# The weight remainders under the norms of the output block: made by VectorE before, by GpSimd now

## What is computed

```python
def layer(x, l):
    h = rms_norm(x, g_pre_mix[l]);  proj = h @ w_in[l]          # window attention and HGRN2 branch
    mixed = concatenate([attn, rec]) @ w_o[l]                   # "wo"
    x = x + rms_norm(mixed, g_post_mix[l])
    mk = rms_norm(mem, g_mem[l]) @ w_xk[l]                      # "memk", 256 memory tokens
    mv = rms_norm(mem, g_mem[l]) @ w_xv[l]                      # "memv"
    q = rms_norm(x, g_pre_x[l]) @ w_xq[l]                       # "xq"
    x = x + rms_norm(cross_attention(q, mk, mv) @ w_xo[l], g_post_x[l])
    x = x + rms_norm(conv_ffn(rms_norm(x, g_pre_ffn[l])), g_post_ffn[l])
```

## Time and profile before

| | |
|---|---|
| median of 3 runs | 4506.29 us (4505.77 to 4507.3) |
| the profiled execution | 4508.9 us |
| its span | 4507.1 us |
| TensorE busy | 3715.9 us, 82% of the span |
| VectorE busy | 2318.1 us, 51% |
| ScalarE busy | 1154.8 us, 26% |
| GpSimd busy | 620.7 us, 14% |
| mean granted clock of TensorE | 0.882 of full speed |
| stretch of the output block in question | about 861 to 963 us in layer 0, 3100 to 3201 us in layer 1 |

### The profile page before, as it was taken

How to read it: one execution, slowest core, us unless ns; L and a number is a source line. 1 busy time by engine, 2 the same in 40 slices (tenths; PEclk the granted TensorE clock), 3 DMA queues, 4 the chain that set the end, 5 groups by cost and what they waited for, 6 DMA issues and landing times. The chain is left out here.

```text
span 4507.1 us, 51872 instructions
## 1 busy us (share of the span) xinstructions
PE 3715.9 (82%) x21568; PEld 3497.0 (78%) x21568; DVE 2318.1 (51%) x3358; ACT 1154.8 (26%) x1608; POOL 620.7 (14%) x254
## 2 busy tenths in 40 slices
PE   6777587987897999999667776879868979999995
PEld 5777474876895999999657765658868959999995
DVE  2555555343005777777725554644330066776676
ACT  3222224423013222222132221344230132122211
POOL 1100011111010122122010000111210102112220
PEclk8888688999588999999878887889985889999998
DMA  2000021221310111111010000112214101111110
GB/s 102 34 29 15 29 53 40 87 71 47 131 45 20 43 52 46 45 43 48 15 49 29 29 29 24 44 56 86 65 38 150 33 18 47 47 43 47 47 51 40
DMA packets 57664, 221.74 MB, mean 49 GB/s; under 512 B 7376, under 2 KB 11856, under 8 KB 52048
## 3 DMA queue, kind: packets, MB, share of 16 engines
q1 hardware_dynamic: 56848, 218.13, 15.1%
q10 hardware_dynamic: 576, 0.24, 0.0%
HBM read 198.47 MB, written 14.59 MB: 47 GB/s over the span
## 5 line engine op out<-in xcount | busy, mean ns | idle before, releaser
L215 PE MATMUL ps<-hh,w_hi 128*128 128x344 f32 (+2 forms) x4320 | 1406.6, 326 | 151.2 <-PEq L361 42.0
L216 PE MATMUL ps<-hl,w_hi 128*128 128x344 f32 (+2 forms) x4320 | 1392.8, 322 | 0.0
L217 PE MATMUL ps<-hh,w_lo 128*128 128x344 f32 (+2 forms) x4320 | 1391.7, 322 | 0.0
L200 POOL TENSOR_TENSOR w_lo<-w_raw,w_hi 128x1024 fp32r<-128x1024 f32 x250 | 620.5, 2484 | 3793.1 <-ACT w_hi L192 3793.0
L215 PEld LDWEIGHTS ps<-hh,w_hi 128*128 128x128 f32 x4320 | 823.4, 191 | 169.7 <-issue 96.0
L216 PEld LDWEIGHTS ps<-hl,w_hi 128*128 128x128 f32 x4320 | 823.6, 191 | 1.1
L217 PEld LDWEIGHTS ps<-hh,w_lo 128*128 128x128 f32 x4320 | 822.8, 190 | 0.0
L1857 DVE TENSOR_TENSOR Y<-Y,ps 128x344 f32<-128x344 f32 x1008 | 476.9, 513 | 168.6 <-PE ps L217 168.6
L192 ACT ACTIVATE w_hi<-w_raw 128x1024 fp32r<-128x1024 f32 x276 | 289.6, 1053 | 931.8 <-PE ps L217 803.0
L215 PE MATMUL ps<-f_ghi,w_hi 128*128 128x344 f32 x1056 | 339.7, 322 | 20.0 <-DVE f_glo L1842 20.0
L217 PE MATMUL ps<-f_ghi,w_lo 128*128 128x344 f32 x1056 | 337.5, 320 | 0.0
(11 more groups left out here) (250 smaller groups left out, 4089.7 us busy)
## 6 DMA issues: line engine op xcount, KB each, us to landing
w_raw<-in_w_stream SPq DMA_DIRECT2D x276, 512.0 KB, 3.6
xs_cache<-in_cache_mem_k SPq DMA_DIRECT2D x16, 1024.0 KB, 5.4
xs_cache<-in_cache_mem_v SPq DMA_DIRECT2D x16, 1024.0 KB, 4.9
xT<-in_x_cols SPq DMA_DIRECT2D x1, 4128.0 KB, 16.8
rope_swapped<-Y SPq DMA_DIRECT2D x32, 129.0 KB, 2.3
out_y_cols<-xT SPq DMA_DIRECT2D x1, 4128.0 KB, 11.2
Y<-in_state_hgrn SPq DMA_DIRECT2D x8, 512.0 KB, 3.7
out_hgrn_sample<-Y SPq DMA_DIRECT2D x8, 512.0 KB, 2.6
```

The lines of the kernel that those rows point to most:

```text
L200: nc.gpsimd.tensor_tensor(w_lo[:, SLOT[m], :], w_raw[:, m % RR, :], w_hi[:, SLOT[m], :].bitcast(F32), ALU.subtract).then_inc(lo_done["pool ...
L215: nc.tensor.matmul(out, whi, mhi, start=start, stop=False)
L216: nc.tensor.matmul(out, whi, mlo, start=False, stop=False)
L217: return nc.tensor.matmul(out, wlo, mhi, start=False, stop=stop)
```

## The change

The list of slabs whose remainders VectorE makes becomes empty, and the thirteen places in VectorE's order go. By the condition in `split_lo`, GpSimd now makes every remainder, in the order of the slabs, and `wait_low` asks GpSimd's semaphore everywhere. Loads, high parts, slots and the order of TensorE and ScalarE stay as they are.

```diff
-LOW_ON_DVE = [m for m in range(len(LOADS)) if VISIT["wo", KT - HR, 1] < LOAD_OF.index(m) < VISIT["xq", 0, 0]]
+LOW_ON_DVE = []
...
-                        def low_slab(i):
-
-                            split_lo_dve(dve, LOW_ON_DVE[i] + 1)
-
...
                         root(0)
-                        low_slab(0)
                         normalise(0)
                         add_post(17)
-                        low_slab(1)
                         residual(0, range(0, 4))
                         add_post(18)
-                        low_slab(2)
                         residual(0, range(4, 8))
```

More of the change, by code:

```diff
@@ L1531, in _ @@
                         root(0)
-                        low_slab(0)
                         normalise(0)
                         add_post(17)
-                        low_slab(1)
                         residual(0, range(0, 4))
                         add_post(18)
-                        low_slab(2)
                         residual(0, range(4, 8))
                         add_post(19)
-                        low_slab(3)
                         root(1)
                         add_post(20)
-                        low_slab(4)
                         normalise(1)
                         add_post(21)
-                        low_slab(5)
                         residual(1, range(0, 4))
                         add_post(22)
-                        low_slab(6)
                         residual(1, range(4, 8))
                         add_post(23)
-                        low_slab(7)
                         low(0, range(0, 4))
                         keys(0)
-                        low_slab(8)
                         low(0, range(4, 8))
                         keys(1)
-                        low_slab(9)
                         low(1, range(0, 4))
                         keys(2)
-                        low_slab(10)
                         low(1, range(4, 8))
                         keys(3)
-                        low_slab(11)
                         keys(4)
-                        low_slab(12)
                         keys(5)
```

## The result

| | median | lowest to highest |
|---|---|---|
| before | 4505.45 us | 4504.62 to 4507.3 |
| with the change | 4525.99 us | 4523.14 to 4527.72 |

The ratio is 1.0043 with a 95% interval of 1.0033 to 1.0054, that is 15 to 24 us slower. The medians lie 20.5 us apart, 4525 was predicted.

The account below looks back on a forecast made before the run. VectorE's queue was taken to bound the stretch; eight blocks of 2.1 us, less removed remainders and waits, make the sum 9.3 us late per layer, nothing after: 4506.29 + 18.6 = 4524.9, said as 4525, range 4510 to 4538.

Parts of the forecast that it names:

- What bounds the stretch: Output block, ahead of the third mean: VectorE's queue, without a break from 866.35 to 896.16 but for 0.49 and 0.73 us.
- The price of a block and their count: VectorE loses 2.1 us per GpSimd turn, eight turns ahead of the third mean's sum in each layer.
- That sum: Sum of squares formerly at 882.72: four blocks cost 8.4 us, VectorE waits 1.6 us, the sum is 5.0 us late.
- The next mark: Sum of squares formerly at 895.73, ahead of TensorE's third mean: at 905.0, 9.3 us late.
- What follows the sum: zero: Slabs 46 to 50 and onward: the ring turns in 7.4 to 7.8 us against 7.61, so nothing is added.
- my upper figure: Ring's turn behind a high part: GpSimd's remainder of 2.4 us plus up to 0.4 for a turn of VectorE.
- the median landing of 3.7 us: Ring's turn: from a remainder's end to the next high part 3.9 us, 3.7 of landing and about 0.2 of issue.
- Rival D: TensorE's clock falls to 1.2 GHz more often after more idleness: +6 to +9 us, 4531 to 4542; chance 0.12.
- the sign that the prediction gave for D: In the profile: the chain as forecast, but TensorE's clock under 0.9 in the stretch.
- A (no turn inside a run): VectorE's runs of residuals: GpSimd gets its turn only at a semaphore; 4506.3 + 16 = 4522; chance 0.15.
- B (relief): VectorE's queue gets shorter, GpSimd's remainders fall under reciprocals and waits: mean 4.7 us sooner, twice, 4496.9; chance 0.06.
- C (half of the turns hidden): Half of the eight fall under reciprocals or PSUM reads: 0.9 us for a layer, 4508; chance 0.10.

Follow-up runs that it names:

- e3_tiny: The changed kernel, but GpSimd subtracts only 8 of 1024 elements for slabs 38 to 50; 0.9953 of the kernel before, -21.2 us.
- e2: Against the kernel before, GpSimd makes the remainders of slabs 38 to 44, VectorE keeps those of 45 to 50; 1.0031, +14.0 us.
- e5: The kernel before, but GpSimd also fills its own tile with zeros three times at each of the thirteen moments; 1.0007, +3.2 us.
- e7: The kernel before, but VectorE also makes the remainders of slabs 25 to 32; 0.9971, -13.1 us.
- e8: The kernel before, but VectorE also makes the remainders of slabs 25 to 32, 54 and 59 to 66; 0.9955, -20.3 us.

## Why the prediction was right

**What bounds the stretch.** Right: every kernel that moved the sum ahead of the third mean moved the kernel the same way (table), and e3_tiny, with neither remainders nor long blocks in VectorE's queue, has the sum 6.9 us sooner. How much of this the queue alone would give stays open.

**The price of a block and their count.** 8 x 2.1 = 16.8 us was reckoned, 16.8 us in eight blocks were read, four on either side of the sum at 888.90, where VectorE waited 1.62 us (1.6 reckoned). That sum comes 22.70 us behind slab 38's high part, 17.66 before: 5.0 late, as reckoned. The next mark is 9.2 us late, 9.3 reckoned; in layer 1 it is 9.2 too.

**What follows the sum: zero.** This term was too small. From slab 46's high part to slab 51's it is 18.6 and 17.9 us where it was 17.5 and 16.8, so +1.1 for each layer. (The 17.5 before is itself high: it was 16.7 to 16.9 in e2, e5, e7 and e8, which leave these slabs as they were.) In the ring's turn from slab 49 to 51, 8.39 us, GpSimd's remainder ended at 926.50, 2.93 us behind its high part, where 2.8 was my upper figure, and from there to the next high part it took 4.40 us and not 3.9. The sum had used the median landing of 3.7 us, and this load is slower in both kernels: it was 4.40 before as well (the VectorE remainder of 913.24 + 1.21 to 918.85). Both times it was issued soon behind another load, by 3.24 and by 2.34 us; that this is the reason is not shown. VectorE's remainder had ended 2.15 us behind its high part, so the turn grew by 2.93 - 2.15 = 0.78 us. The prediction also let VectorE keep a ready slab waiting by up to 1.3 us; for slab 47 it was 2.7 before (from 903.39 to 906.07).

**The clock.** Rival D saw it coming, but not its size. (Its own sum is off: 6 us a layer more makes 4537, not 4531.) Busy time and granted clock of TensorE (the figure behind the five engines; 1.00 is 2.4 GHz, the lower level of 1.2 GHz is 0.50, and what lies between is a mean over the stretch), before and with the change:

```profile
896.00:907.00 11.00, 10.78 (x74) 10.55 (x74) 8.28 (x14) 6.42 (x11) 0.00 (x0) 0.84 0.38 120
907.00:932.00 25.00, 21.97 (x150) 21.05 (x150) 18.52 (x27) 11.78 (x18) 7.36 (x3) 1.00 0.37 118
```

```profile
896.00:908.00 12.00, 8.16 (x49) 7.75 (x49) 11.96 (x13) 2.95 (x5) 6.62 (x3) 0.78 0.53 170
908.00:932.00 24.00, 20.07 (x147) 19.46 (x146) 15.53 (x20) 10.53 (x16) 13.20 (x5) 0.91 0.28 91
```

The granted clock was 0.78 from 896 to 908 and 0.91 from 908 to 932 in layer 0, where before it was 0.84 and 1.00. Ahead of it stood more idleness, TensorE's wait of 9.27 us in place of 2.17. Over 26 us behind 898 it was 0.85, so the sign that the prediction gave for D, under 0.9, did show. The mean's matmuls took 1.25 us in place of 0.71, and from the sum to slab 46 it was 6.20 us in place of 5.66: 0.5 us. A part of the 1.1 us behind slab 46 may be the clock's too; behind the sum it cost at most these 1.6 us a layer, and ahead of the sum VectorE's queue sets the time. D's 6 to 9 us did not come.

**From the stretch to the whole.** 9.2 + 0.5 + 1.1 = 10.8 us a layer make 21.7 before rounding, and the two profiled spans differ by 18.8. What is missing lies in stretches that the change does not touch, above all in one: from slab 24 to slab 38 of layer 1 it was 243.35 us before and 239.79 after. The same stretch gave 239.47 to 243.54 in the experiments that leave it alone, so this is how much executions differ, and no gain of the change. That 4525 met 4526 so closely is luck in part: the terms behind the sum were 1.6 us a layer too low, and such a difference between executions covers it.

**The rivals.** A (no turn inside a run) is excluded by the run at 899.59: its first residual takes 0.61 us, the next two 5.38, with no wait between them. The runs with one block show less: in the one at 875.41 GpSimd's turn falls at the head, and the first residual alone takes 2.75 us. B (relief) is a real force, at the sum at most 6.9 us a layer by e3_tiny, and was outweighed by 16.8 us of blocks. C (half of the turns hidden) fails on the count. The reciprocals hid little: only the first remainder, at 867.34, began under one, and it still blocked the normalise by 2.11.

**Readings.** The overlap at 928.73 ends 0.41 us behind GpSimd's remainder, not 0.45, and GpSimd has five rows between 838 and 963 and not three, since two remainders begin at 961.01. Nothing hangs on either.

## What to carry to other kernels

Work given to an idle GpSimd is not free when VectorE is bound nearby and both read SBUF: each GpSimd instruction that reads SBUF costs VectorE much of its length wherever VectorE works on two SBUF operands, here 2.1 us to save 1.14. Before moving such work, look in the trace for a two-operand VectorE instruction that is longer than its like and ends just behind a GpSimd one, and count how many turns would fall ahead of the wait that matters. The same sight points to work that is better taken back from GpSimd, as e7 and e8 did, though there the shorter instruction has its part too.

## What the runs showed of the hardware

- GpSimd gets its turn between two VectorE instructions of one run, with no semaphore between them: four residuals, 2.20 us when undisturbed, took 4.34 us with one turn and 6.44 with two, and of the latter the first took 0.61 us and the next two 5.38.
- A block costs VectorE 2.0 to 2.1 us of a GpSimd instruction of 2.4, 1.2 to 1.3 of one of 1.9, and 0.95 to 1.05 of a half remainder (1.2).
- The loss is mutual and does not scale with one's own size: of two GpSimd subtractions of 8 elements, 0.20 us undisturbed, the pair took 2.71 us behind a normalise.
- Fills by GpSimd, which read nothing, blocked nothing: from 865 to 919 VectorE's durations were those of before to 0.01 us.
